# Differential attention: memory heads ahead of the differential heads, drain order of the output chunks, and the place of one eviction

## What is computed

```
proj = h @ w_in                       # q 1024, k 1024, v 1024, xq 512 columns
# 8 differential heads: two score matrices each, ALiBi bias, causal
s = einsum(q[c], k[c]) * 64**-0.5     # c = 0, 1: 64 features each
p = softmax(s + bias)
w = p[0] - lam * p[1]
o = rmsnorm(w @ v, norm_g) * (1 - lam_init)
# 4 memory heads of 128 features, 256 memory tokens, no mask
xo = softmax(xq @ mem_k.T * 128**-0.5) @ mem_v
out = concatenate([o, xo]) @ w_out    # 12 tiles of 128 features
```

## Time and profile before

| | |
|---|---|
| median of 3 runs | 1416.6 us |
| profiled execution, its own time | 1417.45 us |
| its span, first to last instruction | 1415.6 us |
| TensorE busy | 1403.5 us, 99% |
| VectorE, ScalarE, GpSimd busy | 857.8, 708.6, 270.1 us |
| granted TensorE clock, mean | 0.997 of full |
| mixer of the change, about | 688 to 825 us of the span |

### The profile page before, as it was taken

One profiled execution on the slowest core, in us unless ns is written; L12 is line 12 of the kernel. 1 busy time (PEld: TensorE's weight loads), 2 busy tenths in 40 slices (PEclk: granted clock), 3 DMA queues, 4 the chain that ended last, 5 costly groups with the idle time before them and its releaser, 6 DMA issues.

```text
span 1415.6 us, 18468 instructions
## 1 busy us (share of the span) xinstructions
PE 1403.5 (99%) x7056; PEld 1185.4 (84%) x7056; DVE 857.8 (61%) x1032; ACT 708.6 (50%) x987; POOL 270.1 (19%) x529
## 2 busy tenths in 40 slices
PE   9999999999999999999999999999999999999998
PEld 7888889888888888888889888888887989888886
DVE  5655566756555565555656665555796655565554
ACT  6555455455444454444565555444555554644443
POOL 1022221102223222222002113222201100132222
PEclk9999999999999999999999999999999999999999
DMA  9756646465655656665544347565554553366562
GB/s 348 286 200 216 205 160 226 151 219 188 220 203 199 216 198 209 211 220 199 182 149 150 132 167 266 205 223 212 177 177 146 189 179 134 125 230 222 197 220 74
DMA packets 73575, 277.12 MB, mean 196 GB/s; under 512 B 18160, under 2 KB 38768, under 8 KB 42768
## 3 DMA queue, kind: packets, MB, share of 16 engines
q1 hardware_dynamic: 58320, 260.35, 52.0%
q0 software_dynamic: 15168, 15.59, 3.7%
HBM read 259.88 MB, written 1.05 MB: 184 GB/s over the span
## 4 chain that ended last, share of the span: by engine, by line
PE 97%; ACT 2%; DVE 1%; DMA 0%; issue 0%; POOL 0%; SPq 0%; DVEq 0%; POOLq 0%; ACTq 0%
PE prod L1220 17%; PE prod L1224 17%; PE prod L1221 17%; PE acc L1224 10%; PE acc L1220 10%; PE acc L1221 10%; PE prod L1214 4%; PE prod L1215 4%; PE prod L1216 4%; PE acc L1421 1%; PE acc L1239 1%; PE acc L1442 1%; ACT w_hi L1577 1%; PE o_bank L1478 0%; PE o_bank L1481 0%; PE prod L1421 0%
## 5 line engine op out<-in xcount | busy, mean ns | idle before, releaser
L1855 DVE TENSOR_TENSOR w_lo<-raw,w_hi 128x2048 fp32r<-128x2048 f32 x233 | 533.6, 2291 | 387.6 <-ACT w_hi L1577 385.2
L1577 ACT CAST w_hi<-raw 128x2048 fp32r<-128x2048 f32 x233 | 444.1, 1907 | 415.6 <-PE prod L1224 188.0
L1220 PE MATMUL prod<-w_hi,acts_h 128*128 128x512 f32 x960 | 376.9, 393 | 2.6 <-DVE w_lo L1864 2.1
L1224 PE MATMUL prod<-w_hi,acts_l 128*128 128x512 f32 x960 | 374.7, 390 | 0.0
L1221 PE MATMUL prod<-w_lo,acts_h 128*128 128x512 f32 x960 | 374.3, 390 | 0.0
L1074 POOL DMA_DIRECT2D four<-four x408 | 200.1, 498 | 607.7 <-DVE four L2016 574.7
L1220 PE MATMUL acc<-w_hi,mix_h 128*128 128x512 f32 x600 | 236.0, 393 | 0.0
L1224 PE MATMUL acc<-w_hi,mix_l 128*128 128x512 f32 x600 | 233.7, 389 | 0.0
L1221 PE MATMUL acc<-w_lo,mix_h 128*128 128x512 f32 x600 | 233.5, 389 | 0.0
L1220 PEld LDWEIGHTS prod<-w_hi,acts_h 128*128 128x128 f32 x960 | 180.7, 188 | 43.3 <-issue 6.4
L1224 PEld LDWEIGHTS prod<-w_hi,acts_l 128*128 128x128 f32 x960 | 180.5, 188 | 38.3 <-DVE acts_l L1926 0.3
(11 more groups left out here) (283 smaller groups left out, 1176.6 us busy)
## 6 DMA issues: line engine op xcount, KB each, us to landing
raw<-in_weights_dram SPq DMA_DIRECT2D x234, 1024.0 KB, 5.0
four<-four SPq DMA_DIRECT2D x408, 16.0 KB, 2.1
four<-four POOLq DMA_DIRECT2D x408, 16.0 KB, 1.8
raw<-in_weights_dram SPq DMA_DIRECT2D x16, 256.0 KB, 6.4
work<-in_mem_dram POOLq DMA_DIRECT2D x2, 1024.0 KB, 12.7
grow<-in_gain_rows_dram POOLq DMA_DIRECT2D x4, 512.0 KB, 3.6
tabs<-in_tabs_dram POOLq DMA_DIRECT2D x1, 1632.0 KB, 10.6
work<-in_x_t_dram SPq DMA_DIRECT2D x4, 256.0 KB, 5.9
```

Source lines behind the costliest of these rows:

```text
L1220: pe.matmul(out, still_hi, wh, start=first, stop=False, skip_group_check=True)
L1224: return pe.matmul(out, still_lo, wh, start=False, stop=last, skip_group_check=True)
L1577: act.copy(w_hi[:, c % RING], raw[:, c % RAW]).then_inc(hi_done, 1)
L1855: dve.tensor_tensor(w_lo[:, c % RING], raw[:, c % RAW], w_hi[:, c % RING].bitcast(F32), ALU.subtract).then_inc(lo_done, 1)
```

## The change

- The memory heads come first in the list of units. Their two query chunks are projected first, the differential pairs behind them.
- The output chunks run in the order of tiles 8-9, 10-11 (memory heads), 0-1, 2-3, 4-5, 6-7; `hold_turn` is gone.
- For the second chunk of a pair of value chunks that has a slot in its middle, ScalarE evicts the first half of the values ahead of the slot, as soon as the first half of the products is done. That holds for both value projections here and two in the last layer.

```diff
--- before.py
+++ after.py
@@ -623,7 +623,7 @@
     heads = [unit_of(h, comps=2, shape=CAUSAL, table="alibi", scale=2.0 ** -(h + 1), q=("q", h), k=("k", h),
                      rows=None, v=("v", h * P), out="norm") for h in range(HEADS)]
     norms = HeadNorms(pl, heads, "diff")
-    ticks = pl.ticks([[unit] for unit in heads + memory])
+    ticks = pl.ticks([[unit] for unit in memory + heads])
     slot = slots(ticks, norms)
 
     def query(pair, mid=slot):
@@ -638,9 +638,18 @@
         end(slot)
         pl.ready_v(heads[2 * pair:2 * pair + 4])
 
-    query(0, None)
+    def memory_query(n, mid):
+        pl.project(w, 3 * D + n * COLS, "xq", 2 * n, mid=mid, factors=(P ** -0.5,) * 2)
+
+    memory_query(0, None)
     pl.spread("x")
-    key(0, None)
+    memory_query(1, None)
+    pl.ready(memory)
+    pl.ready_v(memory)
+    query(0)
+    end(slot)
+    key(0)
+    end(slot)
     pl.ready(heads[0:2])
     value(0)
     query(1)
@@ -655,19 +664,8 @@
         key(pair)
         end(slot)
         pl.ready(heads[2 * pair:2 * pair + 2])
-    for n in range(2):
-        pl.project(w, 3 * D + n * COLS, "xq", 2 * n, mid=slot, factors=(P ** -0.5,) * 2)
-        end(slot)
-    pl.ready(memory)
-    pl.ready_v(memory)
     pl.draining = True
-    norms.hold_turn = True
-
-    def memory_turned(n):
-        if n == 2:
-            norms.hold_turn = False
-
-    downs(slot, "diff_w_out", 0, pairs_of(0, 1, 2, 4, 5, 3), memory_turned)
+    downs(slot, "diff_w_out", 0, pairs_of(4, 5, 0, 1, 2, 3))
     pl.draining = False
     assert next(ticks, "end") == "end"
     assert norms.finished()
@@ -1604,6 +1602,24 @@
                     act.activation(acts_h[:, kt], acc[bank][:, i * S:(i + 1) * S], ACT.Copy,
                                    scale=gain_col(it["gain"], kt)).then_inc(acts_hi, 1)
 
+            def early_value(it):
+                return it["opened"] and it["kind"] == "rows_half" and it["k_half"] and it["dest"] != "rg" and (
+                    it.get("turned") is None)
+
+            def value_half(it, t):
+
+                if t:
+                    act.wait_ge(chunk_used, it["c"] + 1)
+                else:
+                    if it["moved"]:
+                        act.wait_ge(early_features_moved, 128 * it["moved"])
+                        act.wait_ge(late_features_moved, 128 * it["moved"])
+                    act.wait_ge(rstd_done, it["stat"])
+                    act.wait_ge(half_done, it["half"])
+                act.activation(tok_dests[it["dest"]][:, t, it["at"]:it["at"] + 512], prod_flat[(it["e"] + t) % 2],
+                               ACT.Copy, scale=rstd["x" if it["of"] == "x" else "mem"][:, t:t + 1]
+                               ).then_inc(values_read, 1)
+
             def split_piece(c, k):
                 act.wait_ge(piece_loaded[c][k], 16)
                 slot = c % RING
@@ -1616,6 +1632,8 @@
                 kind = it["kind"]
                 if kind in ("open", "hi"):
                     flush()
+                    if kind == "open" and early_value(it["chunk"]):
+                        value_half(it["chunk"], 0)
                 elif kind in ("up", "cols", "rows_half", "down", "group"):
                     if kind != "up" or not it["early_half"]:
                         flush()
@@ -1654,19 +1672,9 @@
                                                          scale=columns_of[k][:, t:t + 1])
                             ins.then_inc(cut_done, 1)
                     elif kind == "rows_half" and it["k_half"]:
-                        if it["moved"]:
-                            act.wait_ge(early_features_moved, 128 * it["moved"])
-                            act.wait_ge(late_features_moved, 128 * it["moved"])
-                        act.wait_ge(rstd_done, it["stat"])
-                        r = rstd["x" if it["of"] == "x" else "mem"]
-                        for t in range(2):
-                            if t:
-                                act.wait_ge(chunk_used, it["c"] + 1)
-                            else:
-                                act.wait_ge(half_done, it["half"])
-                            act.activation(tok_dests[it["dest"]][:, t, it["at"]:it["at"] + 512],
-                                           prod_flat[(it["e"] + t) % 2], ACT.Copy,
-                                           scale=r[:, t:t + 1]).then_inc(values_read, 1)
+                        if not early_value(it):
+                            value_half(it, 0)
+                        value_half(it, 1)
                     elif kind == "up" and it["k_half"]:
                         if it["m"] - 1 in plan.moves and it["m"] % PAIRS:
                             moved_high(it["m"] - 1)
```

## The result

The median went from 1416.57 us to 1420.65 us (7 executions each); the ratio is 1.0029, 95% interval 1.0020 to 1.0038. The forecast was 1420.8, slower. First the page's busy line and the two longest rows of the list of TensorE's waits in the changed kernel, as in the earlier trace rows. Its profiled execution took 1421.6 us, of which the span is 1419.8.

What follows compares the result with a forecast made beforehand. TensorE, busy for 99% of the span, was taken as the bound. The terms -1.12, +0.20 (scores), +0.2 (cuts), +3.28 (wait) and +1.6 (clock) gave +4.2 us, hence 1420.8 us as median; range 1418.5 to 1421.9.

Steps and rivals of the forecast that it cites:

- waits that go: At the value chunks TensorE no longer waits for ScalarE's eviction of the first half: 0.85 and 0.27 us, -1.12 us.
- single scores, cuts: In the drain, heads 6 and 7 scored in four singles of 0.64 us: +0.20; two more cuts of product chunks: +0.2 us.
- new wait on `aux`: Second drained chunk's end: head 6's weights' turn waits for VectorE's low part of turned pair 2, behind ScalarE's cast; +3.28 us.
- clock behind it: Behind the new wait TensorE's granted clock falls once to 0.50, as at the start: +1.6 us.
- rival 1: The new wait on aux stands but the clock does not fall: +2.6, 1419.2 us; chance 0.21.
- Rival 3: At the value chunks ScalarE's evictions stay late, 1.12 us remain lost: 1421.9 us; chance 0.07 together with Rival 4.
- moved memory heads: The memory heads' own chain, moved from the drain to the first slots, runs without a wait: costed at nothing.
- Rival 2: Chain behind head turn 2 runs without the cast in front: growth 1.85, not 3.28; +1.1, 1417.7 us, no change; chance 0.09.
- Rival 4: Last differential pair's head turn or output late again by about 0.85 us: 1421.7 us; chance 0.07 together with Rival 3.

Runs made afterwards that it cites:

- e3_early: The kernel before with only the early eviction of the first half of the values, heads in the old order; 1415.48 us, again 1415.38.
- e4_late: The changed kernel with both halves of the values evicted behind the slot again, new order of heads kept; 1422.03 us.
- e5_fill: The changed kernel with five extra 128x256 products, unused, ahead of the turn of head 6's weights; 1419.71 us.
- e6_twin: e1_hold with the other half's score matrix, unused, beside the single score of head 6's first half; 1417.98 us, again 1417.84.
- e1_hold: The changed kernel with the turn of head pair 2 held back half a chunk, away from the turn of head 6's weights; 1417.22 us, again 1417.23.
- e2_nocast: The changed kernel with ScalarE's cast of the next weights moved behind the head turn's copy, at the second drained chunk's end; 1420.00 us.

## Why the prediction was right, step by step

The sum of the forecast against what the stage measured:

| step | forecast us | measured in the profiled executions, us |
|---|---|---|
| waits that go | -1.12 | -1.24 (e3_early), -1.04 (e4_late) |
| single scores, cuts | +0.40 | +1.32 (what the other rows leave) |
| new wait on `aux` | +3.28 | +3.22 (3.66 less 0.44) |
| clock behind it | +1.6 | +1.60 (e5_fill) |
| sum | +4.2 | +4.90 |

- **The new wait** was right in place, cause and size: the weights' turn came 3.66 us after the head turn against 3.72. TensorE's idle part is 2.22 instead of 2.64 us, below the 2.4 that I had named as its least; half of the difference is the score in between, which lasts 0.85 instead of 0.64.
- **The clock** fell behind it, for eight products as at the start, and e5_fill shows it by taking the idle time away: 1.60 us. (The hole of 1.08 us that I set beside it is a distance between starts; its idle part, to be compared with 2.08 and 2.22, is 0.69 us.) What I had not said is that, as the mean clocks suggest, it does so in some executions and not in others. The five at 1419.8 would then be rival 1 (1419.2), with the scores 0.6 longer.
- **The waits that go** went; the size was right to 0.1 us. Rival 3 is refuted by e3_early and e4_late.
- **The step that failed, in its size: "at the memory head's rate that is 0.86 x 384/512 = 0.64 us".** A single half lasts 0.85 us (796.63 to 797.48 in the changed kernel), as long as a pair; I had taken the rate of 128-row matmuls for 64-row ones. The Trainium skill, page "TensorEngine Tiling (Array Packing)", section "Tiling Modes", says that tiles on different rows run in parallel. The trace of e6_twin agrees: both halves take 0.86 us, one alone 0.84. So a single half costs what a pair costs, the upper bound that I had named and not taken. The four singles cost 4 x 0.85 - 2 x 0.86 = 1.68 us in e1_hold. Its stage is 138.24 - 135.97 = 2.27 us longer than e3_early's, so 0.59 is left, for which I had 0.2 for the cuts and nothing for the moved memory heads. Added up over the rows of both stages, TensorE's other matmuls (scores, turns, outputs) make up 24.86 us in e3_early and 26.54 in e1_hold. That is 1.68 more, the singles' share alone, so the memory heads' matrix work costs the same in its new place. The 0.59 lies in the 690 products, the same number in both, which are cut 28 times instead of 26. How it is spread over the cuts is not worked out here.
- **Why the number still hit.** A fall in every execution would have given 1416.6 + 4.9 = 1421.5; one in none, 1416.6 + 3.3 = 1419.9. The median, 1420.65, lies between; of its seven executions four have a mean clock of 0.998 or less. My scores and cuts were 0.9 us too small, and the clock term, counted in full for every execution, was too large for a median. That the two nearly cancel, so that 1420.8 lies only 0.15 us off, is luck.
- **Rival 2** (the chain without the cast) was not what ran: the cast began at 800.60, 0.25 us after the head turn. Had it been, it would have saved less than I wrote, as e2_nocast shows. Rival 4 (a late last pair) did not appear: within the stage TensorE has no other wait than the 2.2 us and the 0.2 us at its start, and what follows the stage is equal to 0.1 us.

## What to carry to other kernels

When work is reordered, list the users of each shared buffer slot by slot: two steps that never met can land side by side, and the second then waits for the whole chain of the first. On an engine that is 99% busy that wait goes into the time in full, and here the lower clock behind it did too. Here two matrices on opposite halves of the rows cost as much as one, so an order that takes them singly pays twice. Where only single matrices can go, work on all 128 rows loses nothing by it: a memory head's 512 columns took 0.86 us there before. Measure a stage between two marks that every version has: it repeated to 0.04 us where medians moved by up to 0.2.

## What the runs showed that was not expected

- The clock fell behind 2.22 us without a matmul, in a stage where TensorE had been dense, in the three profiles that had that hole; in the profiles of e2_nocast, with 1.48 us, and of the kernel before, with 0.69 us, it stayed full. Filling the hole with useless products saved 1.60 us.
- Taking the longest step out of a chain (1.9 us of cast) shortened it by only 0.73 us, 3.66 to 2.93: the step that had been hidden behind it came next.
